# The last layer's modulation: thirteen of its weight blocks move from TensorE to VectorE's weighted sums

## Chip, cores, metric

One core of one Trainium2 chip runs the whole program in one launch. The metric is device time in microseconds (us) of that core.

## What is computed

Two transformer layers with feed-forwards, then a third one (a "mixer" and a mixture of experts), on 256 tokens of width 1024. Each layer has a modulation: six rows of 1024 factors that come from a condition vector `c` alone, and scale, shift and gate what the norms give.

```python
mod = jax.nn.silu(c) @ w_ada[l] + b_ada[l]          # third layer; c: [1, 1024], w_ada[l]: [1024, 6144]
sh1, sc1, gt1, sh2, sc2, gt2 = [m[:, None, :] for m in jnp.split(mod, 6, axis=-1)]
h = rms_norm_2(x, g_mix[l]) * (1 + sc1) + sh1
...
x = x + gt1 * mix
h2 = rms_norm_2(x, g_ffn[l]) * (1 + sc2) + sh2
x = x + gt2 * hierarchical_moe(h2, ...)
```

The modulation needs nothing of `x`, so its product can be made anywhere in the program before its first use.

## The kernel before

All weights come as blocks of 128 x 2048 numbers (1 MB) in one list, `STREAM`, which SyncE (SP) loads in order (L708). Until the experts begin they share a ring of four buffers: block n may be issued only when block n-4 has been used (`used`, L675). A block of a feed-forward or projection is used when its low parts exist: ScalarE (ACT) writes the high part `whi` (L1546), VectorE (DVE, L2096) and GpSimd (POOL, L1991) write the low part `wlo`, and TensorE (PE) makes each product in three matmuls from high and low parts (L812). POOL writes the low part of the second quarter of a block, DVE the other three, except for the three blocks in `POOL_ALL`, whose four quarters are all POOL's; `("fin", 1, 1)`, the second block of the second feed-forward, is one of them. `whi` and `wlo` hold two blocks.

A third of a layer's modulation is a "set": sets 0 to 2 are the first layer's, 3 to 5 the second's, 6 to 8 the third's. A set has eight blocks `("ada", layer, s, k)`. There are two ways to make it:

- `ada_rows(n, ks)` on PE (L741): four matmuls of 32 columns each for a block (L752), with the condition as the stationary operand, summed over k in bank 7. Sets 0, 1, 2, 6, 7 and 8 are made so.
- `weigh` on DVE (L2121): a block times the condition, added to a sum in SBUF, one instruction of 128 x 2048 for each of two conditions; `ada_sum` (L761) then adds the sum over the partitions in eight matmuls. Sets 3, 4 and 5 are made so, within the first feed-forward, with two blocks in its output half (`ada_fout`).

After either, ACT copies the row (`arow_of`, L1552), PE turns it (`ada_cols`, L769) and DVE adds the bias (`mods`).

The third layer's 24 blocks lie in this order. Set 6: three blocks around the sums of norm 2 (ahead of attention), five between attention's first units (`UNIT_ROWS`). Set 7: three around the sums of norm 3 (ahead of the second feed-forward), five between its blocks 2 to 6 (`after_chunk`). Set 8: four around the sums of norm 4 (ahead of the mixer), four between the mixer's projections. PE fills the rest of each norm with `warm` matmuls on constants (L723), whose results nobody reads.

The output half of a feed-forward has twelve blocks j (the sixth and the twelfth half as long). For each of four steps kk of a block, ACT and DVE split one piece of the hidden values (`high_pair`, then `low_pair`, L2243) into a buffer of two pieces, which PE multiplies two steps later, and split a quarter of the next weight block. What hangs after that (`after_k`) comes last in a step on DVE.

## Time and profile before

| | us |
|---|---|
| median of 3 runs | 1556.65 (1555.0 to 1556.71) |
| the profiled execution | 1556.44 |
| its span, first to last instruction | 1554.5 |
| PE busy in the span | 1470.0 (95%) |
| DVE busy | 775.7 (50%) |
| mean granted clock of PE, share of 2.4 GHz | 0.989 |

The span is the time between the first and the last instruction that the profiler recorded; the execution's own time is 1.9 us longer. PE's records of one fp32 matmul are two, so the four matmuls of one modulation block are eight records. A timeline's row that ends with a bracket says how long the engine had been idle and whose instruction ended that.

### The profile page before, as it was taken

The numbers are of one execution on the slowest core, as the hardware profiler recorded it, in microseconds if no ns is written. First come the engines' busy times: TensorE is split into PE (matmuls) and PEld (weight loads), VectorE is DVE, ScalarE is ACT, GpSimd is POOL, SyncE is SP. The second block draws the span as 40 slices with busy tenths as digits, with TensorE's granted clock in tenths as the row PEclk, the third lists the DMA queues.
The fourth block names the chain that finished last, engine by engine and source line by source line (L and its number), as shares of the span: only waits on it lengthen the run. The fifth ranks groups of instructions, "written<-read, shape, count | busy, mean of one in ns | idle before, by whom it ended". The sixth has DMA issues, their size and how long they took to land.

```text
span 1554.5 us, 21330 instructions
## 1 busy us (share of the span) xinstructions
PE 1470.0 (95%) x8642; PEld 1062.6 (68%) x8642; DVE 775.7 (50%) x1319; ACT 507.2 (33%) x1019; POOL 226.0 (15%) x177
## 2 busy tenths in 40 slices
PE   5999999999999999989999999999999998989987
PEld 3566878878787798878999997898344443334433
DVE  1336866767654887666455667785221211212103
ACT  2324222222344445454444564563111101101102
POOL 0201112121311353002122221230000000000000
PEclk9999999999999999999999999999999999999999
DMA  8693554554423353113765456529899999999994
GB/s 336 281 367 130 210 196 154 208 190 163 148 100 118 136 198 128 55 38 133 274 234 190 150 181 241 188 110 378 359 426 426 426 426 426 427 426 427 426 426 192
DMA packets 54568, 390.51 MB, mean 251 GB/s; under 512 B 6064, under 2 KB 6208, under 8 KB 8000
## 3 DMA queue, kind: packets, MB, share of 16 engines
q1 hardware_dynamic: 53888, 387.72, 63.1%
q8 instruction: 71, 1.16, 0.3%
q10 hardware_dynamic: 576, 1.36, 0.2%
q14 instruction: 33, 0.27, 0.0%
HBM read 388.01 MB, written 1.05 MB: 250 GB/s over the span
## 4 chain that ended last, share of the span: by engine, by line
PE 71%; DMA 19%; DVE 6%; ACT 3%; issue 1%; SPq 0%; DVEq 0%; ACTq 0%
PE twin L812 46%; DMA ring<-in_wblk 18%; PE twin L1391 9%; PE twin L752 2%; PE twin L732 2%; DVE wlo L2096 1%; PE twin L1278 1%; PE twin L1089 1%; PE twin L1379 1%; PE twin L823 1%; PE twin L1025 1%; PE twin L1049 1%; DVE rst L2149 1%; ACT whi L1546 1%; PE twin L1443 1%
## 5 line engine op out<-in xcount | busy, mean ns | idle before, releaser
L2096 DVE TENSOR_TENSOR wlo<-ring,whi 128x512 fp32r<-128x512 f32 (+1 forms) x297 | 260.5, 905 | 142.6 <-ACT whi L1546 141.0
L812 PE MATMUL twin<-Hh,whi 128*128 128x256 f32 (+1 forms) x848 | 281.7, 332 | 8.1 <-DVE wlo L2096 5.8
L1546 ACT ACTIVATE whi<-ring 128x512 fp32r<-128x512 f32 (+1 forms) x408 | 225.1, 611 | 190.0 <-PE twin L812 124.9
L812 PE MATMUL twin<-Hh,wlo 128*128 128x256 f32 (+1 forms) x848 | 279.1, 329 | 0.0
L812 PE MATMUL twin<-Hl,whi 128*128 128x256 f32 (+1 forms) x848 | 279.0, 329 | 0.0
L1991 POOL TENSOR_TENSOR wlo<-ring,whi 128x512 fp32r<-128x512 f32 (+1 forms) x111 | 162.2, 1464 | 754.7 <-ACT whi L1546 754.7
L1391 PE MATMUL twin<-ring,xg 128*64 128x512 f32 x888 | 229.2, 596 | 25.7 <-DMA ring<-in_wblk 21.3
L812 PEld LDWEIGHTS twin<-Hh,whi 128*128 128x128 f32 x848 | 162.8, 192 | 33.2 <-issue 11.0
L1391 PEld LDWEIGHTS twin<-ring,xg 128*64 128x64 f32 x888 | 73.1, 137 | 153.0 <-issue 150.5
L812 PE MATMUL twin<-hsp,whi 128*128 128x512 f32 (+1 forms) x704 | 173.2, 338 | 1.9 <-DVE hsp L2243 1.4
L812 PEld LDWEIGHTS twin<-Hh,wlo 128*128 128x128 f32 x848 | 162.9, 192 | 13.8
L812 PEld LDWEIGHTS twin<-Hl,whi 128*128 128x128 f32 x848 | 163.0, 192 | 13.6
L812 PEld LDWEIGHTS twin<-hsp,whi 128*128 128x128 f32 x704 | 120.7, 190 | 17.8 <-issue 2.2
L2757 DVE TENSOR_TENSOR rst<-rst,twin 128x512 f32<-128x512 f32 x16 | 11.0, 688 | 218.4 <-issue 210.4
L812 PE MATMUL twin<-hsp,wlo 128*128 128x512 f32 (+1 forms) x352 | 118.3, 336 | 0.0
L1391 PE MATMUL twin<-ring,xT 128*64 128x512 f32 x440 | 114.2, 596 | 1.4 <-DMA ring<-in_wblk 1.4
L812 PE MATMUL twin<-whi,Hh 128*128 128x256 f32 x304 | 88.3, 290 | 0.0
L812 PE MATMUL twin<-wlo,Hh 128*128 128x256 f32 x304 | 86.0, 283 | 0.0
L812 PE MATMUL twin<-whi,Hl 128*128 128x256 f32 x304 | 85.9, 283 | 0.0
L2243 DVE TENSOR_TENSOR hsp<-hid,hsp 128x512 fp32r<-128x512 f32 (+1 forms) x88 | 51.8, 593 | 66.7 <-ACT hsp L1649 65.7
L2772 DVE SCALAR_TENSOR_TENSOR outs<-twin,tiny,outs 128x512 fp32r<-128x512 f32 x32 | 24.0, 751 | 104.0 <-ACT outs L1946 52.4
L1649 ACT ACTIVATE hsp<-hid 128x512 fp32r<-128x512 f32 (+1 forms) x88 | 45.5, 524 | 86.4 <-PE twin L812 86.4
(363 smaller groups left out, 2111.8 us busy)
## 6 DMA issues: line engine op xcount, KB each, us to landing
ring<-in_wblk SPq DMA_DIRECT2D x336, 1024.0 KB, 9.0
small<-in_wblk SPq DMA_DIRECT2D x13, 1024.0 KB, 26.1
tmp<-in_wblk SPq DMA_DIRECT2D x13, 1024.0 KB, 26.0
xnat<-in_xnat SPq DMA_DIRECT2D x4, 512.0 KB, 6.8
xT<-in_xin SPq DMA_DIRECT2D x1, 2048.0 KB, 11.0
ring<-in_wblk SPq DMA_DIRECT2D x4, 512.0 KB, 3.8
out<-hTm SPq DMA_DIRECT2D x2, 512.0 KB, 3.0
small<-in_small SPq DMA_DIRECT2D x1, 738.0 KB, 7.7
```

What stands on the lines that cost most here:

```text
L732: t = e.matmul(bank[SUM_BANK[r]][:, 0:n], ones, NORM_SQ[r][:, c, 0:n], start=c == 0, stop=c == KC - 1)
L752: t = e.matmul(bank[7][32 * g:32 * g + 32, :], cact[:, 1 if layer == 2 else 0, k, :], w[:, g * 512:(g + 1) * 512], start=k == 0, stop=k == 7)
L812: t = e.matmul(out, a, b, start=start and n == 0, stop=stop and n == 2)
L823: t = e.matmul(bank[FIRST[c]][:, s * L:(s + 1) * L], xnat[:, 2 * s + t2, c * P:(c + 1) * P], fs[:, 2 * s + t2, :], start=t2 == 0, stop=t2 ...
L1025: t = e.matmul(score_bank(j)[:, c * L2:(c + 1) * L2], qT[pr, h, qt * P:(qt + 1) * P], kT[pr, h, :], start=True, stop=True)
L1391: t = e.matmul(out[64 * i:64 * i + 64, :], lhs(kcs + kk, i), ws[i][:, kk, :], start=start and kk == 0, stop=stop and kk == 3)
L1546: e.activation(hi, w, ACT.Copy).then_inc(*s_hi.up(m, h))
L1649: e.activation(hsp[:, k % nsp, 0, 0:n], hid[:, k, 0:n], ACT.Copy).then_inc(*s_hph.up(layer, half, k))
L1991: e.tensor_tensor(lo, w, hi.bitcast(F32), ALU.subtract).then_inc(*s_log.up(m, h))
L2096: e.tensor_tensor(lo, w, hi.bitcast(F32), ALU.subtract).then_inc(*s_lov.up(m, h))
L2243: e.tensor_tensor(hsp[:, k % nsp, 1, 0:n], hid[:, k, 0:n], hsp[:, k % nsp, 0, 0:n].bitcast(F32), ALU.subtract).then_inc(*s_hpl.up(layer, h ...
L2772: e.scalar_tensor_tensor(osp[:, 1, r], bank[6 + half][:, :], gslot[:, (p - 1) % 2:(p - 1) % 2 + 1], osp[:, 0, r].bitcast(F32), ALU.mult, A ...
```

## The change

- Set 6 and blocks 3 to 7 of set 7 (13 blocks) are weighed by DVE in the first feed-forward's output half, after steps kk = 1 and 3 of the blocks j that `LATE_WEIGHED` names: two blocks in j = 2, 3, 4, 6 and 7, one in 8, 9 and 10. It is one instruction for each, since the third layer has one condition. The first block of each set is a multiplication, the others multiply and add.
- `late_sum` adds the sums over the partitions on PE, four matmuls each: set 6's after block j = 7, set 7's in norm 2, onto what `ada_rows` had summed of its blocks 0 to 2. Set 6's row is turned after j = 9, set 7's at attention's unit 10, where set 6's was.
- In norm 2, `ada_rows(7, 0 to 2)` stands where `ada_rows(6, 0 to 2)` was; three `warm` matmuls follow in place of five, and DVE waits for `late_sum(7)` before the first low part of the norm, whose memory is the sum's.
- In norm 3, `ada_rows(8, 0 to 3)`, four blocks in place of three, and one `warm` in place of three. In norm 4, `ada_rows(8, 4 to 7)` in place of 0 to 3.
- No modulation block is left between attention's units, in the second feed-forward or between the mixer's projections. Their places in `STREAM` change with them.

```diff
+LATE_WEIGHED = {2: [(0, 0), (0, 1)], 3: [(0, 2), (0, 3)], 4: [(0, 4), (0, 5)], 6: [(0, 6), (0, 7)], 7: [(1, 3), (1, 4)], 8: [(1, 5)], 9: [(1, 6)], 10: [(1, 7)]}
+WEIGHED = {3: range(8), 4: range(8), 5: range(8), 6: range(8), 7: range(3, 8)}
...
-    for _after, _s, _ks in ((("din", DIN[1]), 0, range(3)), (("din", DIN[2]), 0, (3,)), (("din", DIN[3]), 0, (4,)), (("din", DIN[4]), 0, (5,)),
-                            (("din", DIN[5]), 0, (6,)), (("din", DIN[6]), 0, (7,)), (("fin", 1, 1), 1, range(3)), (("fin", 1, 2), 1, (3,)), (("fin", 1, 3), 1, (4,)),
-                            (("fin", 1, 4), 1, (5,)), (("fin", 1, 5), 1, (6,)), (("fin", 1, 6), 1, (7,)), (("win", WIN[0]), 2, range(4)),
-                            (("win", WIN[1]), 2, (4,)), (("win", WIN[2]), 2, (5,)), (("win", WIN[3]), 2, (6,)), (("win", WIN[4]), 2, (7,))):
+    if _t[:2] == ("fout", 0):
+        STREAM += [("ada", 2) + x for x in LATE_WEIGHED.get(6 * _t[2] + _t[3] - 1, ())]
+    for _after, _s, _ks in ((("din", DIN[1]), 1, range(3)),
+                            (("fin", 1, 1), 2, range(4)), (("win", WIN[0]), 2, range(4, 8))):
...
+            def late_sum(n):
+                e.wait_ge(*s_adv.at(n, 7))
+                if n == 6:
+                    e.wait_ge(*s_arow.at(5))
+                for g in range(4):
+                    t = e.matmul(bank[7][32 * g:32 * g + 32, :], pick[:, 0, :], late_sums[n - 6][:, g * 512:(g + 1) * 512], start=n == 6, stop=True)
+                t.then_inc(*s_adam.up("sum", n))
...
+                if j == 7:
+                    late_sum(6)
+                if j == 9:
+                    ada_cols(6)
...
-            ada_rows(6, range(2))
+            ada_rows(7, range(2))
             sums(2, range(4, KC))
-            ada_rows(6, range(2, 3))
-            warm(5, 6)
+            ada_rows(7, range(2, 3))
+            late_sum(7)
+            warm(3, 6)
             first_units()
-            UNIT_ROWS = {3: (3,), 5: (4,), 6: (5,), 8: (6,), 9: (7,)}
             for u in range(3, 12):
                 unit(u)
-                ada_rows(6, UNIT_ROWS.get(u, ()))
...
             def around(x):
-                ada_rows(7, range(2, 3) if x else range(2))
+                ada_rows(8, range(2, 4) if x else range(2))
                 if x:
-                    warm(3, 6)
-
-            def after_chunk(p, m):
-                if m and 2 <= p < 7:
-                    ada_rows(7, (p + 1,))
-                if m and p == 9:
-                    ada_cols(7)
+                    warm(1, 6)
...
-            ada_rows(8, range(2))
+            ada_rows(8, range(4, 6))
             sums(4, range(4, KC))
-            ada_rows(8, range(2, 4))
+            ada_rows(8, range(6, 8))
...
             for n in range(1, 5):
                 project(n)
-                ada_rows(8, (n + 3,))
...
+            def late_weigh(n, k):
+                tag, acc_ = ("ada", 2, n - 6, k), late_sums[n - 6][:, :]
+                w, c = block_of(tag), cact[:, 1, k, 0:1]
+                e.wait_ge(*landed(tag))
+                if k > WEIGHED[n][0]:
+                    e.wait_ge(*s_adv.at(n, k - 1))
+                    t = e.scalar_tensor_tensor(acc_, w, c, acc_, ALU.mult, ALU.add)
+                else:
+                    e.wait_ge(*s_wmm.at("fin", 0, 21, 1))
+                    t = e.tensor_scalar(acc_, w, c, None, ALU.mult)
+                t.then_inc(*s_adv.up(n, k))
...
+                    if r == 2 and c == 0:
+                        e.wait_ge(*s_adam.at("sum", 7))
...
+                if kk % 2:
+                    for s, k in LATE_WEIGHED.get(j, ())[kk // 2:kk // 2 + 1]:
+                        late_weigh(6 + s, k)
```

How the order of instructions moves at the places that the prediction speaks of. First DVE in the first feed-forward's output half, blocks j = 2 (its last steps) and 3; `hsp0<-hid0` are the pieces of hidden values, `wlo` the low weights. Before:

```order
L2096 TENSOR_TENSOR wlo<-ring,whi 128x512 [waits weights_high]
L2243 TENSOR_TENSOR hsp0<-hid0,hsp0 128x512 [waits hidden_high]
L2096 TENSOR_TENSOR wlo<-ring,whi 128x512 [waits weights_high]
L2243 TENSOR_TENSOR hsp0<-hid0,hsp0 128x512 [waits hidden_high] x2
L2096 TENSOR_TENSOR wlo<-ring,whi 128x512 [waits weights_high]
```

Now:

```order
L2106 TENSOR_TENSOR wlo<-ring,whi 128x512 [waits weights_high]
L2141 SCALAR_TENSOR_TENSOR late_sum6<-ring,small,late_sum6 128x2048 [waits ada_weighted,ring3_landed]
L2267 TENSOR_TENSOR hsp0<-hid0,hsp0 128x512 [waits hidden_high]
L2106 TENSOR_TENSOR wlo<-ring,whi 128x512 [waits weights_high]
L2267 TENSOR_TENSOR hsp0<-hid0,hsp0 128x512 [waits hidden_high]
L2141 SCALAR_TENSOR_TENSOR late_sum6<-ring,small,late_sum6 128x2048 [waits ada_weighted,ring1_landed]
L2267 TENSOR_TENSOR hsp0<-hid0,hsp0 128x512 [waits hidden_high]
```

Every second piece of hidden values now stands behind a weighing that waits for a landing. Next, PE in norm 3, from the sums of squares (`att,cons`) to the second feed-forward's first matmul. Before:

```order
L732 MATMUL twin2<-att,cons 128x256 [waits squares_act]
L732 MATMUL twin2<-att,cons 128x256 [waits squares_dve]
L752 MATMUL twin3<-ring,small 32x512 [waits ring2_landed]
L752 MATMUL twin3<-ring,small 32x512 x3
L723 MATMUL twin3<-cons 128x512 x3
L812 MATMUL twin0<-Hh1,whi 128x256 [waits normed_low,weights_low_dve]
```

Now:

```order
L737 MATMUL twin2<-att,cons 128x256 [waits squares_act]
L737 MATMUL twin2<-att,cons 128x256 [waits squares_dve]
L757 MATMUL twin3<-ring,small 32x512 [waits ring2_landed]
L757 MATMUL twin3<-ring,small 32x512 x3
L757 MATMUL twin3<-ring,small 32x512 [waits ring3_landed]
L757 MATMUL twin3<-ring,small 32x512 x3
L728 MATMUL twin3<-cons 128x512
L825 MATMUL twin0<-Hh1,whi 128x256 [waits normed_low,weights_low_dve]
```

One more block, with a landing of its own to wait for, stands ahead of the first matmul. Last, SP's queue from attention's blocks into the second feed-forward. A row that waits for `weights_low_pool` alone has a block of `POOL_ALL` four places ahead of it; here it is `("fin", 1, 1)`. Before:

```order
L708 DMA ring<-in_wblk 128x2048 [waits weights_low_pool,weights_low_dve] x10
L708 DMA ring<-in_wblk 128x2048 [waits weights_low_pool]
L708 DMA ring<-in_wblk 128x2048 [waits ada_products] x3
L708 DMA ring<-in_wblk 128x2048 [waits weights_low_pool,weights_low_dve]
L708 DMA ring<-in_wblk 128x2048 [waits ada_products]
```

Now:

```order
L713 DMA ring<-in_wblk 128x2048 [waits weights_low_pool,weights_low_dve] x15
L713 DMA ring<-in_wblk 128x2048 [waits weights_low_pool]
L713 DMA ring<-in_wblk 128x2048 [waits ada_products] x4
L713 DMA ring<-in_wblk 128x2048 [waits weights_low_pool,weights_low_dve] x21
```

Before, the row behind `weights_low_pool` alone was `("fin", 1, 2)`, which is not needed in the norm; now it is the fourth modulation block, `("ada", 2, 2, 3)`, and `("fin", 1, 2)` comes behind it.

## Rows read from the trace of the kernel before

**Rows 1.** The page: engines' busy time, and the chain's shares by engine.

```profile
PE 1470.0 (95%) x8642; PEld 1062.6 (68%) x8642; DVE 775.7 (50%) x1319; ACT 507.2 (33%) x1019; POOL 226.0 (15%) x177
...
PE 71%; DMA 19%; DVE 6%; ACT 3%; issue 1%; SPq 0%; DVEq 0%; ACTq 0%
```

**Rows 2.** ACT's timeline, second feed-forward's input half: start us, us, engine, line, operation.

```profile
763.78 0.38 ACT L1665 ACTIVATE sil<-twin 128x256 f32<-128x256 f32 x1 [0.33 <-PE twin L812]
...
777.66 0.38 ACT L1665 ACTIVATE sil<-twin 128x256 f32<-128x256 f32 x1 [0.44 <-PE twin L812]
...
790.36 0.38 ACT L1665 ACTIVATE sil<-twin 128x256 f32<-128x256 f32 x1 [0.62 <-PE twin L812]
...
802.75 0.38 ACT L1665 ACTIVATE sil<-twin 128x256 f32<-128x256 f32 x1 [1.50 <-PE twin L812]
...
814.27 0.38 ACT L1665 ACTIVATE sil<-twin 128x256 f32<-128x256 f32 x1 [0.62 <-PE twin L812]
...
825.79 0.38 ACT L1665 ACTIVATE sil<-twin 128x256 f32<-128x256 f32 x1 [0.62 <-PE twin L812]
```

**Rows 3.** Timelines of the first feed-forward's output half: DVE, then POOL.

```profile
382.61 3.38 DVE L2121 SCALAR_TENSOR_TENSOR tmp<-ring,small,tmp 128x2048 f32<-128x2048 f32 x1
...
388.63 2.35 DVE L2121 SCALAR_TENSOR_TENSOR stream_sum<-ring,small,stream_sum 128x2048 f32<-128x2048 f32 x1
...
382.55 1.29 POOL L1991 TENSOR_TENSOR wlo<-ring,whi 128x512 fp32r<-128x512 f32 x1 [10.84 <-ACT whi L1546]
393.75 1.28 POOL L1991 TENSOR_TENSOR wlo<-ring,whi 128x512 fp32r<-128x512 f32 x1 [9.91 <-ACT whi L1546]
...
420.15 9.70 POOL L2011 TENSOR_TENSOR tmp<-att 128x128 f32<-128x128 f32 x16
...
456.99 1.28 POOL L1991 TENSOR_TENSOR wlo<-ring,whi 128x512 fp32r<-128x512 f32 x1 [9.54 <-ACT whi L1546]
467.87 1.28 POOL L1991 TENSOR_TENSOR wlo<-ring,whi 128x512 fp32r<-128x512 f32 x1 [9.60 <-ACT whi L1546]
```

**Rows 4.** Busy time in 10 us of attention's units: PE, PEld, DVE, ACT, POOL, clock, DMA.

```profile
560.00:570.00 10.00, 10.00 (x85) 9.03 (x84) 9.15 (x11) 5.40 (x11) 6.49 (x4) 1.00 0.79 316
```

**Rows 5.** PE's timeline in norm 3, ahead of the second feed-forward.

```profile
730.72 1.06 PE L752 MATMUL twin<-ring,small 128*32 128x512 f32 x8
731.72 2.84 PE L723 MATMUL twin<-cons 128*128 128x512 f32 x6
735.09 0.36 PE L812 MATMUL twin<-Hh,whi 128*128 128x256 f32 x1 [0.53 <-DVE Hl L2158]
```

**Rows 6.** Mixer's projections: timelines of PE and DVE, then stretches with busy times and clock.

```profile
973.89 0.56 PE L812 MATMUL twin<-Hh,whi 128*128 128x256 f32 x1 [3.98 <-DVE wlo L2096]
...
982.87 0.38 PE L812 MATMUL twin<-whi,Hh 128*128 128x256 f32 x1
...
973.06 1.88 DVE L2096 TENSOR_TENSOR wlo<-ring,whi 128x512 fp32r<-128x512 f32 x3
...
970.00:974.00 4.00, 0.11 (x1) 0.14 (x1) 3.89 (x7) 2.19 (x4) 1.37 (x1) 0.72 0.67 250
974.00:980.00 6.00, 6.00 (x34) 6.00 (x35) 5.79 (x10) 0.00 (x0) 0.00 (x0) 0.62 0.53 186
```

**Rows 7.** SP, one 1 MB block's issue in the output half, and its landing.

```profile
L708 SPq DMA_DIRECT2D ring<-in_wblk x1: 327/327/327, 424.7 to 424.7; - x1
...
DMA to landing us min/median/max: 4.7/4.7/4.7
```

**Rows 8.** Norm 3: POOL's timeline; SP's waits (total, times, longest); DMA issues and landings.

```profile
728.58 4.96 POOL L1991 TENSOR_TENSOR wlo<-ring,whi 128x512 fp32r<-128x512 f32 x4 [5.91 <-ACT whi L1546]
...
SPq L708 <- POOL wlo L1991: 9.4, 1, 9.4
...
L708 SPq DMA_DIRECT2D ring<-in_wblk x2: 327/376/424, 733.6 to 733.9; - x2
...
DMA to landing us min/median/max: 4.8/6.5/8.1
```

More of the change, by code:

```diff
@@ L240, in program @@
         ffn_memory(0)
+        late_sums = (own("late_sum6", [P, BW]), own("hole", [P, BW]), own("late_sum7", [P, BW]))[::2]
+        give_back(2)
         AH = (own("Hh", [P, KC, L2], F32R), own("Hl", [P, KC, L2], F32R))
@@ L393, in program @@
         for n, (layer, s) in enumerate(SETS):
-            mine = [[("sum", n)]] if layer == 1 else [[(n, k)] for k in range(8)]
+            mine = [[(n, k)] for k in range(8) if k not in WEIGHED.get(n, ())] + [[("sum", n)]] * (n in WEIGHED)
             mine[-1].append(("rows", n))
@@ L397, in program @@
         s_adam = signal("ada_products", events)
-        s_adv = signal("ada_weighted", [(n, k) for n in (3, 4, 5) for k in range(8)])
+        s_adv = signal("ada_weighted", [(n, k) for n in WEIGHED for k in WEIGHED[n]])
         s_arow = signal("ada_rows", [(n,) for n in range(9)])
@@ L557, in turned_rows @@
         def turned_rows(n):
-            return bank[{0: 7, 6: 5}.get(n, 6)]
+            return bank[{0: 7, 7: 5}.get(n, 6)]
         def unit_turned(u):
@@ L676, in used @@
                 if tag[0] == "ada":
-                    signal = s_adv if tag[1] == 1 else s_adam
-                    e.wait_ge(*signal.at(3 * tag[1] + tag[2], tag[3]))
+                    n = 3 * tag[1] + tag[2]
+                    signal = s_adv if tag[3] in WEIGHED.get(n, ()) else s_adam
+                    e.wait_ge(*signal.at(n, tag[3]))
                 else:
@@ L752, in ada_rows @@
                         t = e.matmul(bank[7][32 * g:32 * g + 32, :], cact[:, 1 if layer == 2 else 0, k, :], w[:, g * 512:(g + 1) * 512],
-                                     start=k == 0, stop=k == 7)
+                                     start=k == 0, stop=k == 7 and n not in WEIGHED)
                     t.then_inc(*s_adam.up(n, k))
@@ L1106, in pe @@
                 if u == 10:
-                    ada_cols(6)
+                    ada_cols(7)
             value_tile(0)
-            e.wait_ge(*s_mod.at(6, 0))
+            e.wait_ge(*s_mod.at(7, 0))
             e.wait_ge(*s_uk.at(9))
@@ L1158, in after_block @@
                     sums(4, range(4))
-            ffn(1, around, after_chunk, after_block)
+            ffn(1, around, lambda p, m: None, after_block)
             def project(n, ms=range(2)):
@@ L1686, in early2 @@
                     e.dma_start(rope, rope_d).then_inc(s_rope_in, 16)
+                if j == 7:
+                    arow_of(6)
                 if j in (8, 9):
@@ L1714, in act @@
                 if u == 10:
-                    arow_of(6)
+                    arow_of(7)
                 e.wait_ge(*s_wmm.at(*unit_block(u), UNITS[u][2]))
@@ L1796, in early4 @@
                     square(4, a, lambda c: e.wait_ge(*s_fx.at(1, c, 0)))
-            ffn(1, lambda c: e.wait_ge(*s_ax.at(c)), lambda: None, lambda p: arow_of(7) if p == 8 else None, early4)
+            ffn(1, lambda c: e.wait_ge(*s_ax.at(c)), lambda: None, lambda p: None, early4)
             def project(n):
@@ L2290, in ada_fout @@
                     weigh(22 + j, kk // 2)
+                if kk % 2:
+                    for s, k in LATE_WEIGHED.get(j, ())[kk // 2:kk // 2 + 1]:
+                        late_weigh(6 + s, k)
                 if (j, kk) == (5, 0):
                     mods(5)
+                if (j, kk) == (10, 3):
+                    mods(6)
                 if j in (8, 9) and kk == 3:
@@ L2339, in dve @@
                 if u == 10:
-                    mods(6)
+                    mods(7)
             def maxima(j):
@@ L2435, in early4 @@
                     square(4, 2 * j - 15, lambda c: e.wait_ge(*s_fx.at(1, c, 0)))
-            ffn(1, None, lambda p, m: mods(7) if (p, m) == (10, 1) else None, early4)
+            ffn(1, None, lambda p, m: None, early4)
             def project(n):
```

## The prediction

> **What bounds the kernel now.** I read the page first. PE is busy for 95% of the span and DVE for half of it, and the chain that ended last is PE for 71% and DMA for 19% [rows 1]. So a change that takes work from PE pays where PE's queue is the bound, and only there. The stretches differ, so I went by timelines, place by place. In the second feed-forward's input half PE never waits: ACT's gate activations, which each follow a PE block, come evenly, and that spacing prices what stands between the blocks [rows 2]. In the first feed-forward's output half PE runs without a pause too, but DVE already weighs two blocks there, so the price of a weighing can be read [rows 3]. In attention's first units PE is full and DVE nearly so [rows 4]. In the norms PE fills time [rows 5]. In the mixer's projections PE waits for DVE [rows 6]. Behind the mixer comes the experts' stream, whose start is released by the mixer's end: what comes earlier there ends earlier, so gains ahead of it are kept.
>
> **The price of a modulation block on PE.** Two gates of the same chunk kind lie 13.88 us apart (763.78 to 777.66) with two blocks between, and 11.52 us (814.27 to 825.79) with none: 1.18 us a block. Turning a row costs 12.39 - 11.52 = 0.87 us (790.36 to 802.75) [rows 2].
>
> **Term 1, second feed-forward.** Five blocks and one turning go: -(5 x 1.18 + 0.87) = -6.8 us, all on PE's path.
>
> **Term 2, attention's units.** Five blocks go, -5.9 us at the same price; a turning of units follows most of them and shares the switch, so I take 1.1 each, -5.5. PE then needs a unit some 1 us sooner while DVE, 9.15 busy of 10 us, splits the weights [rows 4]; I give back 1.0, between 0 (PE stays the bound) and 3 (DVE's whole rest of 0.85 in 10 us over some 60 us is 5, of which PE asks for less). -4.5 us. The row's turning stays where it was.
>
> **Term 3, the mixer's projections.** Four blocks go, 4.7 us of PE. But PE waits 3.98 us for the low weights there, and DVE starts those at 973.06, straight behind its own work [rows 6]: two of the four blocks stand before that wait and only lengthen it. The other two stand before waits that DVE and ACT set. I take 0; the ends are -2.4 (the two behind) and +0.5.
>
> **Term 4, first feed-forward's output half.** PE gains a sum, four matmuls like a block's, 1.2 us, and a turning, 0.9. DVE gains 13 weighings of 2.35 us (the two that only multiply are shorter), 29 us. The half already shows what they do [rows 3]: a weighing after step kk = 1 begins at 382.61, just behind POOL's split at 382.55, and takes 3.38 us; the one after kk = 3 takes 2.35. A block with two of them paces at 11.20 us (POOL's splits, 382.55 to 393.75), one without at 10.88 (456.99 to 467.87): 0.32 us a block, all from the kk = 1 place. Eight blocks get a weighing there; in j = 2 and 7 it is the short one. Six remain, one of which (j = 3) meets POOL's rotation tables, 9.70 us of short operations. Five at 0.32 are 1.6; for j = 3 I take 1.0 (0.3 if the tables did not matter, 3 if both its weighings were held up as the one at 382.61 was). The ring matters too: in j = 4, 7 and 8 the weighing's block may be issued only when the split of the block before is done, 10 us into that block; it lands 4.7 us later [rows 7], 3.9 us into the next, which is when DVE comes to it. No wait, but no room. Sum: 1.2 + 0.9 + 1.6 + 1.0 = +4.7 us (3.5 to 9).
>
> Here the rows show that the operation that begins second is the one stretched. The Trainium skill ("SBUF — State Buffer", Who interferes with whom) says that VectorE, when it reads two inputs from SBUF, and GpSimd share a port pair as an exclusive lock: whichever starts first holds it for the whole instruction. By that rule a weighing at the tables waits for one table operation at most (9.70 us by 16, 0.6), so that j = 3 would cost 0.6 in place of my 1.0 and the term 4.3; I keep 1.0, since the two sums differ by less than the bounds, and the 3.38 us row is 1.03 us over 2.35, about as long as the rule's lock by the 1.29 us split would be.
>
> **Term 5, norm 2.** `late_sum(7)` takes 1.0 us, two `warm` matmuls that go gave 1.9. DVE's new wait is for a sum that ends about 3 us before DVE's first low part. 0, hidden under the norm.
>
> **Term 6, norm 3: a new wait.** The norm's fourth modulation block, `("ada", 2, 2, 3)`, is issued only when `("fin", 1, 1)`, four places ahead, has its low parts. Those are POOL's four quarters, 728.58 to 733.54; SP waits for just that, 9.4 us, and issues at 733.6; the first of that burst lands 4.8 us later, 738.4 [rows 8]. PE is through with the third block at 731.7, and in today's kernel starts the first product at 735.09, after `warm` to 734.56 [rows 5]. In the changed one PE stands before the fourth block until 738.4, needs 1.0 for it and 0.95 for the one `warm`: first product at 740.4, 5.3 us later. Nothing runs past it: PE's queue is in order, and from 735 on PE was the bound. After 6.7 idle us PE's clock will be low. The nearest row: after the idle 3.98 us ahead of 973.89 the granted clock was 0.72, then 0.62 of full, that is partly at 1.2 GHz, and the projection with its one block took 8.98 us (to 982.87) where half of 13.88 is usual: 2.0 us lost [rows 6]. Bounds: 0 if the clock holds, 3.5 if it stays low for longer. +5.3 + 2.0 = +7.3 us.
>
> This stands on the burst landing in the order of issue, as 4.8 and 8.1 us for its first two show; if the fourth block came as the second did, it would be 3.3 us more.
>
> Norm 4 keeps four blocks with the same releases: 0.
>
> **Sum.** -6.8 - 4.5 + 0 + 4.7 + 0 + 7.3 = +0.7 us on 1556.4 (span and what lies around it): 1557.1; against the median of the runs, 0.2 higher, **1557.3**. A measurement of this kernel tells about 0.2%, 3.1 us, from no change. The forecast's own range is 1553.5 to 1562, from the terms' ends.
>
> **Rivals.**
>
> A, *faster: the norm covers the fourth block*. If its landing is no later than the norm, terms 1 and 2 stay, term 6 is 0 and the time is 1557.3 - 7.3 = **1550.0**. For it: the change puts the block where PE only warmed up. Against it: SP's wait and issue at 733.6 are rows. It decides if the release comes before about 729. 13%.
>
> B, *slower: the output half breaks*. The weighing at kk = 1 waits for its landing. It decides once a landing takes more than about 6.2 us instead of 4.7: then DVE is late with the next piece of hidden values, and PE, which has only two, stops. At 1.5 us in each of j = 4, 7 and 8 and 2 at the tables, with clock and everything else as forecast, that (1.0 of it is in term 4) is 5.5 more: **1562.8**. For it: blocks now come two at a time. Against it: the landing read there is 4.7 [rows 7]. 20%.
>
> C, *faster: the projections pay*. PE, not DVE, sets the pace there and the four blocks are worth 4.7: **1552.6**. Against it: the 3.98 us wait [rows 6]. 8%.
>
> **How the numbers follow.** Forecast 59%, A 13%, B 20%, C 8%. The lines are at 1553.5 and 1559.8. Of the forecast about 6 points lie below the lower and 11 above the upper; of C 3 and of B 2 fall between them. Faster: 13 + 5 + 6 = 24%; slower: 18 + 11 = 29%; within: 42 + 3 + 2 = 47%. The range from 1551.5 to 1563.5 leaves out most of A and the tail of B, together under 20%.
>
> **What would show it.** In the changed profile: PE idle for some 6 us before the second feed-forward, released by a DMA; a granted clock under 1 right behind; two-chunk gates at 11.5 us throughout that half; output-half blocks of 11.2 us; the mixer's wait for DVE grown by 2 us. It is wrong if that idle time is absent, if the output half grows by over 9 us, or if the projections shrink.

## The result, and the profile of the changed kernel

| | us |
|---|---|
| kernel before, median of 7 runs on this chip | 1556.03 (1554.55 to 1556.83) |
| changed kernel, median of 7 runs | 1564.65 (1560.16 to 1565.43) |
| ratio | 1.0041, 95% interval 1.0029 to 1.0053 |
| the changed kernel's profiled execution, and its span | 1564.87, 1563.1 |

The change makes the kernel 0.41% slower, 6.4 us on 1556.65, that is 1563.0. The ratio is not that of the two medians in the table, which lie further apart: 8.6 us, or 1.0055. A second set of runs on another chip gave 1.0059 (1.0037 to 1.0080). The profiled execution is 8.6 us longer in its span. I had forecast +0.7 us. Its page says that PE does less and waits more: its busy time fell from 1470.0 to 1461.8 us, while DVE gained 35.5.

```profile
PE 1461.8 (94%) x8546; PEld 1062.6 (68%) x8546; DVE 811.2 (52%) x1332; ACT 507.1 (32%) x1019; POOL 233.8 (15%) x177
...
PE 67%; DMA 19%; DVE 8%; ACT 3%; issue 2%; POOL 1%; SPq 0%; DVEq 0%; ACTq 0%
```

The program's order is fixed, so both traces can be laid beside each other at instructions that they share. I cut them at nine such starts and took the length of each stretch, after less before:

| stretch, from the start of ... to the start of ... | before | change |
|---|---|---|
| output half of the first feed-forward: PE's sum of set 5 to norm 2's reciprocal | 99.89 | +8.26 |
| norm 2: to POOL's first operation of the units | 23.45 | +0.93 |
| attention's units: to POOL's last operation of them | 66.54 | -3.88 |
| rest of attention: to norm 3's reciprocal | 129.74 | +1.62 |
| norm 3: to the second feed-forward's first gate | 11.72 | +7.32 |
| its input half: to the last gate | 120.17 | -6.77 |
| output half, norm 4, projections: to POOL's first sum in the mixer | 127.63 | +0.01 |
| rest of the mixer: to the experts' first `cons,rst` matmuls on PE | 112.84 | 0.00 |
| experts: to the last norm's sums on PE | 437.96 | +1.21 |

The sum is +8.70; the changed trace is 0.06 us early where the first stretch begins, which makes the 8.64 us between the last marks (1541.66 and 1550.30). The first 411.7 us, ahead of the first mark, are in no stretch.

**Norm 3** went as forecast. PE's timeline, then stretches with busy times, granted clock, DMA share and GB/s, then SP's waits:

```profile
737.59 1.06 PE L757 MATMUL twin<-ring,small 128*32 128x512 f32 x8
745.35 1.94 PE L757 MATMUL twin<-ring,small 128*32 128x512 f32 x8 [6.70 <-DMA ring<-in_wblk]
747.22 2.08 PE L728 MATMUL twin<-cons 128*128 128x512 f32 x2
748.31 1.20 PE L825 MATMUL twin<-Hh,whi 128*128 128x256 f32 x1
```

```profile
742.00:744.00 2.00, 0.00 (x0) 0.00 (x0) 2.00 (x6) 1.19 (x3) 0.00 (x0) 0.80 0.86 344
744.00:746.00 2.00, 0.65 (x4) 0.20 (x8) 2.00 (x6) 1.35 (x3) 0.00 (x0) 0.50 1.02 430
...
748.00:750.00 2.00, 2.00 (x7) 1.25 (x6) 0.00 (x0) 0.01 (x1) 0.00 (x0) 0.50 1.04 438
750.00:755.00 5.00, 5.00 (x43) 5.00 (x43) 0.00 (x0) 0.00 (x0) 0.00 (x0) 1.00 0.92 385
```

```profile
SPq L713 <- POOL wlo L2001: 9.4, 1, 9.4
```

PE stands 6.70 us for a DMA, SP waits the same 9.4 us for POOL as in [rows 8], and the block and the `warm` matmul behind the wait take 1.94 and 2.08 us in place of 1.06 and about 0.95, at a granted clock of 0.50, the 1.2 GHz level. The first product comes 6.35 us later than before, counted from the norm's start: 5.3 us for the wait and 1.0 for the slow clock ahead of it. The other 1.0 us is lost behind it, by 750.

**The second feed-forward** also went as forecast. ACT's gates lie 11.52 us apart from the start (compare [rows 2]):

```profile
766.97 0.38 ACT L1674 ACTIVATE sil<-twin 128x256 f32<-128x256 f32 x1 [2.50 <-PE twin L825]
778.49 0.38 ACT L1674 ACTIVATE sil<-twin 128x256 f32<-128x256 f32 x1 [2.50 <-PE twin L825]
790.01 0.38 ACT L1674 ACTIVATE sil<-twin 128x256 f32<-128x256 f32 x1 [2.50 <-PE twin L825]
```

**The output half** did not. Here are timelines around the rotation tables, to be read beside [rows 3]: POOL before (the row ahead of the tables and two behind them), then POOL, DVE and PE of the changed kernel.

```profile
419.21 0.85 POOL L2002 TENSOR_SCALAR att<-att 128x256 f32<-128x256 f32 x1
...
429.81 0.74 POOL L1991 TENSOR_TENSOR wlo<-ring,whi 128x256 fp32r<-128x256 f32 x1
...
446.11 1.33 POOL L1991 TENSOR_TENSOR wlo<-ring,whi 128x512 fp32r<-128x512 f32 x1 [7.24 <-ACT whi L1546]
```

```profile
421.22 0.85 POOL L2012 TENSOR_SCALAR att<-att 128x256 f32<-128x256 f32 x1 [2.03 <-DMA att<-in_rope]
422.15 16.61 POOL L2021 TENSOR_TENSOR tmp<-att 128x128 f32<-128x128 f32 x16
438.72 2.87 POOL L2001 TENSOR_TENSOR wlo<-ring,whi 128x256 fp32r<-128x256 f32 x2
451.09 1.34 POOL L2001 TENSOR_TENSOR wlo<-ring,whi 128x512 fp32r<-128x512 f32 x1 [9.51 <-ACT whi L1555]
```

```profile
424.42 2.54 DVE L2141 SCALAR_TENSOR_TENSOR late_sum<-ring,small,late_sum 128x2048 f32<-128x2048 f32 x1
...
429.65 2.54 DVE L2141 SCALAR_TENSOR_TENSOR late_sum<-ring,small,late_sum 128x2048 f32<-128x2048 f32 x1
...
435.90 2.54 DVE L2141 SCALAR_TENSOR_TENSOR late_sum<-ring,small,late_sum 128x2048 f32<-128x2048 f32 x1
```

```profile
422.31 0.70 PE L825 MATMUL twin<-hsp,whi 128*128 128x512 f32 x2 [0.29 <-DVE hsp L2267]
...
439.99 1.19 PE L825 MATMUL twin<-hsp,whi 128*128 128x512 f32 x2 [2.78 <-issue]
```

DVE is hardly late: PE waits 0.29 us for it once, and is 0.8 us behind the kernel before when it has multiplied the last piece of that block. The victim is POOL. Its 16 table operations take 16.61 us in place of 9.70, three weighings lie in them (the second of j = 3 and both of j = 4), and POOL's low quarter of the next weight block, which is queued behind the tables, begins at 438.72 in place of 429.81. Of these 8.9 us 6.9 are the longer tables, and 2.0 have another cause: the tables begin later. Their own input, `in_rope`, is loaded beside the weight blocks that the change brought to this place (2.56 MB of them move between 412 and 420, in place of 1.05). It lands 7.4 us after its issue in place of 3.5 (the first line is the kernel before, the second the changed one), and POOL waits 2.03 us for it:

```profile
att<-in_rope ACTq DMA_DIRECT2D x1, 512.0 KB, 3.5
...
att<-in_rope ACTq DMA_DIRECT2D x1, 512.0 KB, 7.4
```

PE resumes at 439.99, after 2.78 us for which the trace names no releaser ("issue"). A later quarter shows the price: at 446.11 before and at 451.09 now, 4.98 us later; until the tables the two traces ran within 0.1 us. The other 3.2 us come in small parts as forecast, 1.23 at the block with set 6's sum and 1.27 at the block with its turning among them.

### The profile page after: what moved, and what is told of

Same layout as the page of the kernel before. It is cut to its first block, busy times and chain, and to the rows that moved or that the text cites. A ratio compares the mean times of both kernels' runs of the same rounds, so it can differ in the third digit from the quotient of the medians.

```text
span 1563.1 us, 21165 instructions
## 1 busy us (share of the span) xinstructions
PE 1461.8 (94%) x8546; PEld 1062.6 (68%) x8546; DVE 811.2 (52%) x1332; ACT 507.1 (32%) x1019; POOL 233.8 (15%) x177
## 3 DMA queue, kind: packets, MB, share of 16 engines
HBM read 388.01 MB, written 1.05 MB: 249 GB/s over the span
## 4 chain that ended last, share of the span: by engine, by line
PE 67%; DMA 19%; DVE 8%; ACT 3%; issue 2%; POOL 1%; SPq 0%; DVEq 0%; ACTq 0%
PE twin L825 44%; DMA ring<-in_wblk 19%; PE twin L1400 9%; DVE wlo L2106 2%; PE twin L757 2%; PE twin L737 1%; PE twin L1288 1%; PE twin L1388 1%; PE twin L1042 1%; PE twin L836 1%; ACT whi L1555 1%; PE twin L1066 1%; PE twin L1106 1%; PE twin L1452 1%; DVE rst L2171 1%
## 5 line engine op out<-in xcount | busy, mean ns | idle before, releaser
L1400 PEld LDWEIGHTS twin<-ring,xT 128*64 128x64 f32 x440 | 35.1, 136 | 57.2 <-issue 57.0
```

The costliest lines, as they stand in the source:

```text
L1400: t = e.matmul(out[64 * i:64 * i + 64, :], lhs(kcs + kk, i), ws[i][:, kk, :], start=start and kk == 0, stop=stop and kk == 3)
```

## The experiments

The expectations were on record before each run. The first four kernels below shared a chip; the two unchanged kernels, the three repairs and the repairs with `warm` shared another; the short weighings, the small matmuls and the last two shared a third. Runs scattered more on these chips (1554.15 to 1562.52 for the kernel before beside the first four), so ratios are uncertain by 0.1% and more, and the parts are read from the stretches. Each profile is one execution, sometimes the fastest or the slowest of its kernel's runs, so its total is not the median.

**Three blocks in norm 3 again.**

```diff
-                            (("fin", 1, 1), 2, range(4)), (("win", WIN[0]), 2, range(4, 8))):
+                            (("fin", 1, 1), 2, range(3)), (("fin", 1, 2), 2, (3,)), (("win", WIN[0]), 2, range(4, 8))):
...
-                ada_rows(8, range(2, 4) if x else range(2))
+                ada_rows(8, range(2, 3) if x else range(2))
                 if x:
-                    warm(1, 6)
+                    warm(3, 6)
...
-            ffn(1, around, lambda p, m: None, after_block)
+            ffn(1, around, lambda p, m: ada_rows(8, (3,)) if (p, m) == (2, 1) else None, after_block)
```

> Theory (the fourth modulation block in norm 3 waits for the ring slot that the second block of the second feed-forward holds until POOL's last low quarter): with three blocks and three warm matmuls in the norm again, and the fourth block on PE between two blocks of the second feed-forward, PE's idle 6.70 us before that feed-forward and the slow clock behind it go (7.3 us), the block costs 1.2 us where it now stands: 6.1 us less than the changed kernel, so about 0.3 us over the kernel before. Rival (the norm is as long as before and PE was short of something else there, for example the sums or the normed values): PE waits again, by 4 us or more, and the time hardly falls.

Measured: ratio 1.0008 (0.9998 to 1.0017). Norm 3 takes +0.02 us in place of +7.32, the feed-forward's input half -5.59 in place of -6.77: a block is 1.18 us, and the first product waits 0.54 us as before. So the two stretches give back the 6.1 us that the theory named; the ratio is some 1 us above the 0.3 us over the kernel before that I expected, with the mixer's clock and the experts in it (table below).

**The order of loads.**

```diff
-                            (("fin", 1, 1), 2, range(4)), (("win", WIN[0]), 2, range(4, 8))):
+                            (("fin", 1, 0), 2, (0,)), (("fin", 1, 1), 2, range(1, 4)), (("win", WIN[0]), 2, range(4, 8))):
```

> Four blocks stay in norm 3, but in the list of loads the first of them goes ahead of the feed-forward's second block, so that the fourth is released by the first modulation block (used some 5 us before POOL's last low quarter). Theory (the slot's release is the cause): it is issued about 5 us earlier and lands about when PE comes to it; PE's idle time there falls from 6.70 us to 0 to 2, the clock stays high, 6 to 7 us less than the changed kernel, about 0 to -1 us against the kernel before. Rival (four 1 MB blocks cannot land in the norm whatever their order, since they share the DMA engines with the feed-forward's own blocks): PE still waits 4 us or more, and at most 3 us are gained.

Measured: ratio 1.0010 (1.0000 to 1.0020); norm 3 +0.03 us. PE's timeline in norm 3:

```profile
734.27 1.06 PE L757 MATMUL twin<-ring,small 128*32 128x512 f32 x8
736.36 1.07 PE L757 MATMUL twin<-ring,small 128*32 128x512 f32 x8 [1.03 <-DMA ring<-in_wblk]
737.36 1.13 PE L728 MATMUL twin<-cons 128*128 128x512 f32 x2
738.65 0.36 PE L825 MATMUL twin<-Hh,whi 128*128 128x256 f32 x1 [0.17 <-DVE Hl L2182]
```

Four blocks do fit into the norm: the wait falls from 6.70 to 1.03 us and the norm covers it. The rival with the shared DMA engines is out. What cost 7.3 us was one ring slot's release, not a fourth block. The time itself, 1.0010, is above the 0 to -1 us that I had expected against the kernel before: the other stretches keep their losses.

**No weighing in j = 3.**

```diff
-LATE_WEIGHED = {2: [(0, 0), (0, 1)], 3: [(0, 2), (0, 3)], 4: [(0, 4), (0, 5)], 6: [(0, 6), (0, 7)], 7: [(1, 3), (1, 4)], 8: [(1, 5)], 9: [(1, 6)], 10: [(1, 7)]}
+LATE_WEIGHED = {2: [(0, 0), (0, 1)], 4: [(0, 2), (0, 3)], 6: [(0, 4), (0, 5)], 7: [(0, 6), (0, 7)], 8: [(1, 3), (1, 4)], 9: [(1, 5), (1, 6)], 10: [(1, 7)]}
```

> The two weighings of output block j = 3 go to later blocks (j = 4, 6, 7, 8 two each, 9 two, 10 one), the number of weighings stays 13. Theory (DVE's weighings stretch POOL's 16 table operations from 9.70 to 16.61 us, POOL's low quarter of the next block comes late behind them, and PE waits 2.78 us and loses clock): the tables run in about 10 us again, PE's wait goes, 3.5 to 4.5 us less than the changed kernel. Rival (it is the mere number of weighings on DVE in a row): the loss moves to j = 8 and 9, where DVE now has two each, and the time stays within 1.5 us.

Measured: ratio 1.0013 (1.0002 to 1.0025). The output half costs +5.55 us in place of +8.26, a gain of 2.7, less than the 3.5 that I expected. The tables take 11.83 us, since one weighing of j = 4 still meets them, and PE's long wait is gone, although they begin late here too (POOL waits 2.80 us for `in_rope`). A new wait came: set 6 is now finished late in j = 7, and PE's sum stands for it.

```profile
466.75 1.06 PE L774 MATMUL twin<-late_sum,pick 128*32 128x512 f32 x8 [1.33 <-DVE late_sum L2141]
```

**The tables in two halves.**

```diff
             for table, source, o in ((rotA, "cosr", 0), (rotB, "sinr", 128)):
...
+                if i and o == 0:
+                    split(BLK["fout", 0, 0, 5] + 1)
```

> All weighings stay where they are; only POOL's queue is changed: its low quarter of the next weight block goes between the first eight and the last eight table operations. Theory (PE's wait comes from POOL's quarter behind the stretched tables): the tables still take some 16 us in all, but PE's wait of 2.78 us and the slow clock behind it go, 3 to 4 us less than the changed kernel. Rival (DVE is late at j = 3 and 4 for its own five weighings): PE waits as before at the same place, now for DVE, and the time stays within 1 us.

Measured: ratio 1.0012 (0.9999 to 1.0024), the output half +5.16 us, 3.1 less. POOL's timeline:

```profile
422.54 7.89 POOL L2023 TENSOR_TENSOR tmp<-att 128x128 f32<-128x128 f32 x8
430.40 2.78 POOL L2001 TENSOR_TENSOR wlo<-ring,whi 128x256 fp32r<-128x256 f32 x1
433.15 7.62 POOL L2023 TENSOR_TENSOR tmp<-att 128x128 f32<-128x128 f32 x8
```

The tables are nearly as slow as in the changed kernel, 15.5 us for 16.61, and begin as late, with all weighings in their places, yet the loss is gone, because the quarter that PE needs no longer stands behind them. PE's waits in this half are 0.30, 0.51 and 0.41 us, all for DVE's hidden pieces. The two theories of this place are told apart: it was POOL's queue, not DVE's lateness.

**Short weighings.**

```diff
-                    t = e.scalar_tensor_tensor(acc_, w, c, acc_, ALU.mult, ALU.add)
+                    t = e.scalar_tensor_tensor(acc_[:, 0:64], w[:, 0:64], c, acc_[:, 0:64], ALU.mult, ALU.add)
```

> The changed kernel with eleven of the thirteen weighings cut to 64 of 2048 columns (the two multiplications that begin a set stay whole); all loads, waits, sums and turnings stay. It leaves out most of the modulation's third layer, sets 6 and 7. Theory (DVE's time and its hold on POOL cost the output half 6 of its 8.3 us; the ring and the loads cost nothing): the tables take about 10 us again and the half costs +2.1 to +2.7 us (sum 1.2, turning 0.9). Rival (landings and ring slots hold the half up): +4 us or more stays.

This kernel leaves out most of the arithmetic of sets 6 and 7. Measured: ratio 1.0006 (0.9996 to 1.0016), the output half +2.18 us, and the tables:

```profile
421.67 8.80 POOL L2021 TENSOR_TENSOR tmp<-att 128x128 f32<-128x128 f32 x16
```

All loads and ring slots are the same. 2.1 us were forecast for the sum and the turning, so landings and slots by themselves cost next to nothing there, and the weighings' time on DVE accounts for 8.26 - 2.18 = 6.1 us. The tables' late load is here too (POOL waits 1.37 us for it), and the quarter behind them still comes early enough. In the changed kernel both add up: PE waits 2.78 us for a quarter that is 2.0 us later by the load alone, so with that load on time perhaps 0.8 us of the wait would be left, an estimate. No run takes the late load away by itself.

**The two kernels again, unchanged.**

> The kernel before, unchanged, for a second profile. The first set of experiments differed from the profile of before in places where their code is the same: 1.2 us between the second expert pair and the end in all of them, and by -1 to +4.6 us in attention and in the mixer at a changed clock. Theory (that the clock falls at other moments in each execution): this profile differs from the first one by up to 4 us in attention, in the mixer or behind it, with the same waits of PE. Rival (the changed kernels cause these differences): it repeats the first profile within 0.3 us in every stretch, the 1.2 us at the end included.

> The changed kernel, unchanged, on the chip of the combined kernels, for a second profile and a ratio there. Expected: first feed-forward's output half +8.2 us, norm 3 +7.3 us, second feed-forward -6.8 us again within 0.3 us; norm 2, attention and the mixer by up to 4 us otherwise than in the first profile; ratio to the kernel before 1.003 to 1.005.

Measured: 1.0000 (0.9986 to 1.0014) and 1.0059 (1.0037 to 1.0080). The kernel before differs from its own first profile by +0.92 us in norm 2, +1.79 in attention and +1.20 in the rest of the mixer, and by 0.08 or less in the other six stretches, the experts included. It is also 2.19 us longer ahead of the first mark, which comes between 409.4 and 413.9 us in the fourteen profiles, although at most two weighings were added there. So the theory holds for the first three, the rival for the experts: their 1.2 us come with the change. The changed kernel repeats its first profile within 0.07 us in every stretch, where I had expected other values for norm 2, attention and the mixer, and its ratio is above the expected 1.003 to 1.005. Norm 2 in the second profile of the kernel before:

```profile
519.80 0.36 PE L1089 MATMUL twin<-whi,Hh 128*128 128x256 f32 x1 [1.27 <-DVE Hl L2158]
...
521.30 0.58 PE L1089 MATMUL twin<-whi,Hh 128*128 128x256 f32 x1 [0.55 <-DVE Hl L2158]
```

In the first profile the same two waits, 1.27 and 0.55, were followed by 0.36 and 0.39 us matmuls; here the second takes 0.58, at the lower clock: granted 0.66 in 520 to 525, and 1.00 in the same five us of the first profile (517.8 to 522.8). The same work and the same waits give either clock.

**Three repairs at once**, and then with matmuls between the projections. The first takes the new order of loads, the halved tables and, in norm 2, `warm(5, 6)` for `warm(3, 6)`. The second and third add:

```diff
 for n in range(1, 5):
     project(n)
+    warm(1, 4)
```

```diff
 for n in range(1, 5):
     project(n)
+    for _ in range(12):
+        e.matmul(bank[4][:, 0:8], ones, cons[:, 0:8], start=True, stop=True)
```

> Three repairs at once: the order of loads that frees norm 3's fourth block early (-7.3 us), POOL's table operations in two halves (-3.1), and five warm matmuls in place of three in norm 2, so that PE's idle time there falls from 2.1 to about 0.3 us (0 to -0.9, by whether the clock falls there). Against the changed kernel -10.4 to -11.3 us, so 3 to 5 us faster than the kernel before (ratio 0.997 to 0.998). Rival (what the repairs free is lost again to the clock in the mixer, where PE waits 6.2 and 3.4 us in place of 4.0 and 1.5): the first part of the profile gains as said, but the ratio is 0.999 or more.

> The same three repairs, and a warm matmul behind each of the mixer's projections 1 to 4, where the kernel before had modulation blocks of the same length. Theory (the waits of PE there cost nothing by themselves, but the low clock behind them does): PE's waits are 4.0 and 1.5 us again, the stretch from norm 4 to the experts is within 0.5 us of the kernel before, and the whole is 1 to 2 us faster than without the warm matmuls in the median, with less scatter. Rival (the removed blocks cost and gave nothing there): the same time as without them within 1 us.

> The three repairs again, and twelve matmuls of 8 columns behind each of the mixer's projections 1 to 4: 96 records of PE in the place where PE waits, as many as the change took from PE before the experts. In all profiles with the change the last 1 MB block that goes to the buffer `tmp` lands 30.3 us after its issue, in both profiles of the kernel before 29.2, and the end comes 1.2 us later; an instruction fetch of 16 KB lies in its last few us in the first and not in the second. Theory (the fetch comes when PE passes a certain number of instructions, so the count before the experts sets where it falls): with the count restored the block lands in 29.2 us and the stretch from the second expert pair to the end is 393.7 us again, 1.2 less than the same kernel without them. Rival (something else of the change sets it): it stays 394.9.

Measured: 0.9989 (0.9976 to 1.0003), 0.9994 (0.9981 to 1.0007) and 0.9991 (0.9979 to 1.0002). By the profiles the repairs are worth what they should be (output half +5.12, +5.12, +5.31; norm 2 +0.02 each; norm 3 0.00 to +0.01). The ratio of the first, 0.9989, lies short of the 0.997 to 0.998 that I expected, and its interval reaches from one side's number to the other's, so between theory and rival it does not decide. With `warm` between the projections PE's two waits there are 4.64 and 2.25 us in place of 6.16 and 3.40, and norm 4 to the experts is within 0.2 us of the kernel before, as the theory said; but the time is no lower than without them, and there the rival was right.

The small matmuls did what they were made for at the end, once. The blocks' issues and landings (KB, us to landing), in the changed kernel and in this one:

```profile
tmp<-in_wblk SPq DMA_DIRECT2D x1, 1024.0 KB, 30.3
```

```profile
tmp<-in_wblk SPq DMA_DIRECT2D x1, 1024.0 KB, 29.1
```

The experts' stretch is -0.01 us here, as before the change. Between 1525.45 and 1529.45 the changed kernel has an instruction fetch among its DMA transfers, as below; at the same point of the program, 1518 to 1522 in the kernel before and 1518.44 to 1522.44 in this one, there is none:

```profile
q8 instruction: 1, 0.02, 1.5%
```

In the kernel before (both profiles) and in this one the last fetch comes 8 us ahead of the last mark, when the last block has landed.

**Everything together.** The first kernel below has no weighing in j = 3, the halved tables, the new order of loads, `warm(5, 6)`, and set 6's sum and ACT's copy after j = 8; the second has the small matmuls too.

```diff
-                if j == 7:
+                if j == 8:
                     late_sum(6)
...
-                if j == 7:
+                if j == 8:
                     arow_of(6)
```

> The three repairs, and in addition no weighing in output block j = 3 (they move to later blocks as in the earlier experiment), with set 6's sum and its copy one block later, after j = 8, so that PE does not wait for the last weighing. Expected: the output half costs +3.7 to +4.5 us over the kernel before, in place of +5.1, so 0.6 to 1.4 us faster than the combined kernel. Rival (two weighings in j = 8 and 9 bring the same stalls there): +5.1 again.

> Everything together: order of loads, halved tables, no weighing at j = 3, set 6's sum later, five warm matmuls in norm 2, twelve small matmuls behind each of projections 1 to 4. Expected by the parts: 2 to 2.5 us faster than the three repairs alone, ratio to the kernel before 0.996 to 0.998. Rival (clock falls in attention and the mixer take it back): ratio 0.999 or more.

Measured: 0.9978 (0.9963 to 0.9992) and 0.9977 (0.9968 to 0.9987), about 3.5 us faster than the kernel before, and 10 to 13 us faster than the changed one by its two ratios (these come from other chips). The output half costs +4.06 and +4.08, 1.1 less than with the three repairs. In the second the theory of the fetch held only half: its `tmp` block lands in 29.1 us, but the last ring block takes 28.1 in place of 26.6, and the experts' stretch is +1.37 again. Its last fetch lies between 1530.4 and 1530.9, behind the landing of the block before (26.4 us after its issue at 1503.0) and ahead of the landing of the last (28.1 after 1505.1). So the same 96 records put the last fetch at two different places, but in both kernels, as in all the others, just those of the last blocks are late that land behind it.

The stretches of all profiles, less the kernel before's first (us):

| | before again | after | after again | three in norm | order | clear of tables | halved | short weighings | repairs | with warm | with small | clear and halved | all |
|---|---|---|---|---|---|---|---|---|---|---|---|---|---|
| output half | 0.00 | 8.26 | 8.25 | 8.41 | 8.32 | 5.55 | 5.16 | 2.18 | 5.12 | 5.12 | 5.31 | 4.06 | 4.08 |
| norm 2 | 0.92 | 0.93 | 0.91 | 0.01 | 0.01 | 0.95 | 0.93 | 0.89 | 0.02 | 0.02 | 0.02 | 0.01 | 0.01 |
| units | -0.01 | -3.88 | -3.88 | -3.87 | -3.88 | -3.87 | -3.88 | -3.88 | -3.90 | -3.91 | -3.87 | -3.88 | -3.88 |
| rest of attention | 1.79 | 1.62 | 1.62 | 0.64 | 0.66 | 1.48 | 1.57 | 1.48 | 0.66 | 0.00 | 3.39 | -0.07 | -0.13 |
| norm 3 | 0.01 | 7.32 | 7.25 | 0.02 | 0.03 | 7.00 | 7.24 | 6.97 | 0.01 | 0.00 | 0.00 | 0.01 | 0.01 |
| input half | 0.00 | -6.77 | -6.77 | -5.59 | -6.77 | -6.77 | -6.77 | -6.77 | -6.77 | -6.77 | -6.77 | -6.77 | -6.77 |
| to the mixer | 0.04 | 0.01 | 0.02 | 0.03 | 0.03 | 0.01 | 0.02 | 0.04 | 0.03 | 0.22 | 0.19 | 0.00 | 0.24 |
| rest of the mixer | 1.20 | 0.00 | -0.01 | 4.58 | 1.18 | -0.02 | -0.01 | -0.53 | 1.23 | -0.03 | 2.18 | 0.60 | 5.70 |
| experts | -0.07 | 1.21 | 1.28 | 1.24 | 1.22 | 1.27 | 1.19 | 1.14 | 1.11 | 1.21 | -0.01 | 1.18 | 1.37 |

Six rows go by the edit, and where the edit is the same they repeat within 0.35 us; the output half's is the sum of its parts. Three (norm 2, the rest of attention, the rest of the mixer) are set by when the clock falls, and the last two of these range over 3.5 and 6.2 us.

## Why the prediction was right and wrong

Its range, up to 1563.5, held the time of 1563.0, barely; the plain median of the seven runs, 1564.65, lies above it. Its likeliest case, no change, did not come, and slower had 29%. The narrower range, 1553.5 to 1562, was said to come from the terms' ends and does not: these add up to 1550.7 to 1565.6.

**Right.** Term 1: -6.8 forecast, -6.77 measured. Term 6: +7.3 forecast, +7.32 measured, with the idle time (6.70), its releaser and the slow clock behind it as said, and the order of loads shows the cause. That the price of the slow clock, 2.0 us, came out so closely is luck: it was taken from another place, with bounds of 0 and 3.5. Term 3: 0 forecast, +0.01 to the mixer's first sum. PE's wait for DVE's low weights grew from 3.98 [rows 6] to 6.18 us, by about the two blocks that had stood before it:

```profile
981.31 0.55 PE L825 MATMUL twin<-Hh,whi 128*128 128x256 f32 x1 [6.18 <-DVE wlo L2106]
```

So rival C is out. Rival A fell too as the change stands, but the new order of loads shows that it named the place rightly: the norm covers the block once its slot is free. Term 2: -4.5 forecast, -3.88 measured, within its bounds. If the blocks were worth the assumed 5.5 us, the give-back to a full DVE is 1.6 in place of 1.0; no run takes the two apart.

**Wrong: term 4**, +4.7 forecast, +8.26 measured, within its bounds (up to 9). The step that failed is "for j = 3 I take 1.0", with a loss of 3 at most "if both its weighings were held up". The place cost 5.0 us, of which 1.3 were in the sum (0.3 for j = 4). I had priced what the tables do to the weighing and not what the weighings do to the tables, nor what stands behind the tables in POOL's queue. The trace of before had it: POOL's low quarter at 429.81 follows the 9.70 us of tables at once, and the change's weighings lie beside them in j = 3 and j = 4, of which I counted j = 3 alone. The trace shows 6.91 us of stretch, about three weighings of 2.35. The tables' own load, delayed by 2.0 us by the new loads beside it, was in no term either. And the two multiplications are not shorter, as I had written: they take 2.33 us. That they cost nothing at the kk = 1 place has another reason, shown at the end.

The rule of the Trainium skill ("SBUF — State Buffer", Who interferes with whom) agrees with that: the engine that comes second is blocked for the whole instruction, whichever of the two it is. By it three weighings of 2.35 us among short table operations hold POOL for some 7.1 us, an estimate from the row's duration, and 6.91 were measured. I had applied it to DVE only.

Rival B gave nearly the measured time, but for another cause: no instruction of DVE waits for a DMA in that half, and with the loads kept and the weighings cut short only 2.18 us are left. Where the new loads do hurt, in the 2.0 us of the tables' input, it is POOL that waits.

**Wrong: term 5 and what no term covered.** Norm 2 was to cost 0 and costs 0.9 where the clock falls there, which it did in five of the seven profiles with three `warm` matmuls there, and in none of the five with five. The idle time there is 2.13 us in place of 1.27. The kernel before had the loss in one of two profiles, so only a part is the change's. The experts' +1.2 was in no term; it comes with the change in eleven of twelve profiles and is the late landing of the last blocks. That instruction fetches set it is likely: one kernel moved the last fetch behind all landings and lost the delay, another moved it between the last two and had the last block late. Why a fetch of 0.02 MB should cost over 1 us, and what sets its place, stays open. Attention's 1.6 us need not be the change's: the unchanged kernel shows 0 in one profile and 1.79 in the other.

Without the three stretches in which the clock falls at other moments, the change is worth -3.88 + 8.26 + 7.32 - 6.77 + 0.01 + 1.21 = +6.2 us, close to the 6.4 of the ratio. The forecast's terms for the same rows gave +0.7; of the 5.5 us between them 3.6 are term 4, 1.2 the experts, 0.6 the units.

## What to carry to other kernels

When work moves to DVE beside GpSimd operations that read SBUF, price both sides: how much later the other engine's queue gets, and what stands in that queue that TensorE needs. Putting the needed operation ahead of the long run of operations was worth as much as taking the work away (3.1 and 2.7 us). Where a load ring hands out slots in a fixed order, look at which block frees the slot of a load that is needed early; exchanging two entries of the list gave back 7.3 us, with the same work in the same place. And ask which other load a moved block will delay: here it was the tables' input, by 3.9 us.

## What the runs showed of the hardware

- The granted clock can fall or hold behind the same waits. In norm 2 waits of 1.27 and 0.55 us were followed by full speed in one profile and by the 1.2 GHz level in another, for 0.92 us. In the rest of attention and of the mixer such falls are worth from -0.1 to +3.4 and from -0.5 to +5.7 us, more than most edits here; a single profile cannot judge an edit of a few us by its total, while in the repeated profiles of both kernels the other stretches of the table agree within 0.1.
- With all 16 DMA engines busy, one block of the stream landed in 30.3 us where it took 29.2 before the change, at the same point of the program; an instruction fetch (0.02 MB) lies just ahead of the later landing. Of the blocks that land in the last 20 us, those that land behind the last fetch come 0.9 to 1.5 us late in all fourteen profiles, and no others: with the fetch 22 us ahead of the last mark (ten profiles) the `tmp` block and the ring blocks behind it (27.8 for 26.6), with 12 us the last ring block alone (28.1), with 8 us none. Earlier fetches are in every profile too, one of them always 31 to 34 us ahead of the mark, and what those cost cannot be read here.
- Short weighings, DVE then POOL:

```profile
418.07 1.32 DVE L2141 SCALAR_TENSOR_TENSOR late_sum<-ring,small,late_sum 128x64 f32<-128x64 f32 x1
...
434.73 0.28 DVE L2141 SCALAR_TENSOR_TENSOR late_sum<-ring,small,late_sum 128x64 f32<-128x64 f32 x1
```

```profile
418.03 1.28 POOL L2001 TENSOR_TENSOR wlo<-ring,whi 128x512 fp32r<-128x512 f32 x1 [11.71 <-ACT whi L1555]
```

A weighing cut from 2048 to 64 columns took 1.32 us at 418.07, beside a 1.28 us POOL operation that had begun at 418.03, and 0.28 us at 434.73 with POOL idle: a short operation waits for the other engine as long as a long one does.
- One input or two. In the changed kernel the first weighing of a set, which multiplies a block by a number and so reads one tensor, begins like the others just behind POOL's split, and is not held up; the one that also reads its sum is (2.35 us without POOL). DVE, then the POOL operations that they meet:

```profile
404.94 2.33 DVE L2144 TENSOR_SCALAR late_sum<-ring,small 128x2048 f32<-128x2048 f32 x1
...
417.94 3.39 DVE L2141 SCALAR_TENSOR_TENSOR late_sum<-ring,small,late_sum 128x2048 f32<-128x2048 f32 x1
```

```profile
404.90 1.29 POOL L2001 TENSOR_TENSOR wlo<-ring,whi 128x512 fp32r<-128x512 f32 x1 [9.91 <-ACT whi L1555]
...
417.90 1.29 POOL L2001 TENSOR_TENSOR wlo<-ring,whi 128x512 fp32r<-128x512 f32 x1 [11.71 <-ACT whi L1555]
```
